# The first two-job unit of an expert stage gets the loop's fourteen steps, its pair products in the first step and its slots from a table

## What is computed

```
def moe_swiglu(hn, router_w, w1, w3, w2):
    ...
    logits = (t @ router_w).astype(jnp.float32)
    top_v, top_i = lax.top_k(logits, TOP_K)          # TOP_K = 2 of 8
    gates = jax.nn.softmax(top_v, axis=-1)
    ...
    for e in range(N_EXPERTS):
        out = out + gate_te[:, e:e + 1] * swiglu(t, w1[e], w3[e], w2[e])
```

## Time and profile before

| | us |
|---|---|
| median of 3 runs | 1252.86 |
| lowest, highest | 1252.4, 1255.4 |
| profiled execution | 1251.35 |
| its span | 1249.6 |
| first matmul of an expert unit | 403.75 from the span's start |

### The profile page before, as it was taken

How to read it: one execution, slowest core, us unless ns; L and a number is a source line. 1 busy time by engine, 2 the same in 40 slices (tenths; PEclk the granted TensorE clock), 3 DMA queues, 4 the chain that set the end, 5 groups by cost and what they waited for, 6 DMA issues and landing times.

```text
span 1249.6 us, 16988 instructions
## 1 busy us (share of the span) xinstructions
PE 1219.5 (98%) x6506; PEld 874.2 (70%) x6506; DVE 710.3 (57%) x854; ACT 576.8 (46%) x608; POOL 20.0 (2%) x54
## 2 busy tenths in 40 slices
PE   8999999999999999999999999999999999999997
PEld 7688999999879765556655655575655666565654
DVE  5976666654553755555554642664545646464645
ACT  2266656533564652444354441634445444454443
POOL 3200000000000000000000000000000000000000
PEclk9999999999999999999999999999999999999999
DMA  9433555523075789999999999999999999999993
GB/s 388 183 149 133 173 181 186 201 101 135 2 301 208 266 331 423 421 421 421 421 421 420 421 420 422 420 422 421 421 420 421 422 421 421 421 420 422 420 422 142
DMA packets 58019, 411.83 MB, mean 330 GB/s; under 512 B 6241, under 2 KB 6369, under 8 KB 9697
## 3 DMA queue, kind: packets, MB, share of 16 engines
q1 hardware_dynamic: 57776, 410.68, 80.8%
q10 hardware_dynamic: 144, 0.26, 0.1%
q0 software_dynamic: 32, 0.00, 0.0%
HBM read 409.87 MB, written 1.05 MB: 329 GB/s over the span
## 4 chain that ended last, share of the span: by engine, by line
PE 81%; DMA 7%; DVE 6%; ACT 3%; issue 2%; SPq 1%; DVEq 0%; ACTq 0%
PE banks L1144 21%; PE banks L1116 10%; PE banks L1117 10%; PE banks L838 9%; PE banks L1119 9%; DMA raw<-in_exp_dram 6%; PE banks L853 5%; DVE low L2135 3%; PE banks L728 2%; PE banks L954 2%; PE banks L773 2%; PE banks L1089 2%; PE banks L742 1%; ACT squares L1468 1%; PE banks L1124 1%
## 5 line engine op out<-in xcount | busy, mean ns | idle before, releaser
L2135 DVE TENSOR_TENSOR low<-raw,high 128x2048 fp32r<-128x2048 f32 x165 | 374.4, 2288 | 157.6 <-ACT high L1526 157.2
L1526 ACT ACTIVATE high<-raw 128x2048 fp32r<-128x2048 f32 x165 | 313.6, 1913 | 305.8 <-DMA raw<-in_exp_dram 169.1
L1144 PE MATMUL banks<-raw,x_full 128*64 128x512 f32 x896 | 198.1, 595 | 1.9 <-ACT x_full L1536 1.9
L1116 PE MATMUL banks<-high,x_high 128*128 128x512 f32 x448 | 179.2, 400 | 2.0 <-DVE low L2135 2.0
L1119 PE MATMUL banks<-high,x_low 128*128 128x512 f32 x448 | 174.6, 390 | 0.0
L1117 PE MATMUL banks<-low,x_high 128*128 128x512 f32 x448 | 174.4, 389 | 0.0
L1144 PEld LDWEIGHTS banks<-raw,x_full 128*64 128x64 f32 x896 | 62.3, 137 | 121.0 <-issue 121.0
L1144 PE MATMUL banks<-raw,h_full 128*64 128x512 f32 x448 | 102.3, 598 | 0.0
L1116 PEld LDWEIGHTS banks<-high,x_high 128*128 128x128 f32 x448 | 84.1, 188 | 21.1 <-DVE low L2135 3.8
L1116 PE MATMUL banks<-high,h_high 128*128 128x512 f32 x224 | 92.0, 411 | 5.6 <-DVE low L2135 4.3
L1117 PEld LDWEIGHTS banks<-low,x_high 128*128 128x128 f32 x448 | 84.2, 188 | 18.2 <-issue 1.4
(11 more groups left out here) (312 smaller groups left out, 1592.4 us busy)
## 6 DMA issues: line engine op xcount, KB each, us to landing
raw<-in_exp_dram SPq DMA_DIRECT2D x336, 1024.0 KB, 19.4
raw<-in_ff_dram SPq DMA_DIRECT2D x33, 1024.0 KB, 4.7
weights<-in_w_in_conv_dram SPq DMA_DIRECT2D x4, 1024.0 KB, 10.2
weights<-in_w_out_dram SPq DMA_DIRECT2D x2, 2048.0 KB, 25.4
weights<-in_w_qkv_dram SPq DMA_DIRECT2D x1, 4096.0 KB, 18.0
weights<-in_w_o_dram SPq DMA_DIRECT2D x1, 4096.0 KB, 12.2
weights<-in_w_in_pool_dram SPq DMA_DIRECT2D x1, 2048.0 KB, 19.1
weights<-in_w_qkv_dram SPq DMA_DIRECT2D x1, 2048.0 KB, 8.2
```

The lines of the kernel that those rows point to most:

```text
L1116: pe.matmul(dst, own_high[:, i, :], high[:, slot, w], start=first, stop=False)
L1144: mm = pe.matmul(PS[rows, bank, :], own[:, k, rows], raw[:, raw_slot[at[t]], w], start=first, stop=last)
L1526: act.activation(high[:, k % SPLIT, :], raw[:, raw_slot[at], :], ACT.Copy).then_inc(high_ready, 1)
L2135: dve.tensor_tensor(low[:, k % SPLIT, :], raw[:, raw_slot[full_at(p, job.side * UNITS + k)], :], high[:, k % SPLIT, :].bitcast(F32), ALU.s ...
```

## The change

The opening is gone. `prelude` is removed from PE, ACT and DVE, the first duo uses LOOP_STEPS like every other, and `ups` has a branch for the first job, which has no earlier job to bring back: it turns its own selection after the first unit and gathers the pair's tokens after the fourth. The first duo's steps 0 and 1 thus hold pair units of group 0.

The loads of the first duo are no longer in the order of the products. The first sixteen are still full units 0 to 15 (OPENING = 16), because the pair's experts aren't known; then come all others in the products' order. A table, `first_places`, gives each unit its slot: load i takes the slot of the unit that stands at place i - 14 of the products' order. It also counts how often each slot was filled, for the waits. The loop gets its own table, which goes on from the slots where the first duo ends. Apart from this, ten warm-up matmuls are added at the kernel's start, four between the transposes of the input and six behind them.

```
-    FIRST_STEPS = [(0, 2, None, 0), (0, 3, 0, 1), (0, 4, 1, None), (0, 5, None, 2), (0, 6, 2, None),
-                   (1, 0, None, 3), (1, 1, 3, None), (1, 2, None, 4), (1, 3, 4, None), (1, 4, None, 5),
-                   (1, 5, 5, 6), (1, 6, 6, None)]
     LOOP_STEPS = [(s // GROUPS, s % GROUPS, s // 2 if s % 2 else None, None if s % 2 else s // 2)
                   for s in range(2 * GROUPS)]
...
+    opening = [("full", k) for k in range(OPENING)]
+    first_loads = opening + [unit for unit in joint if unit not in opening]
+
+    def first_places():
+        slots, turns, count = {}, {}, [0] * RAW
+        for i, unit in enumerate(first_loads):
+            s = i if i < RAW else slots[joint[i - RAW]]
+            count[s] += 1
+            slots[unit], turns[unit] = s, count[s]
+        return [slots[unit] for unit in joint], [turns[unit] for unit in joint], count
...
+            def load_first():
+                full_jobs = [0]
+                for t in range(RAW, len(first_loads)):
+                    unit = first_loads[t]
+                    if t == OPENING:
+                        sp.wait_ge(pairs_ready, 1)
...
+                    wait_gone(FIRST_DUO, *joint[t - RAW])
+                    load_one(unit, first_slots[joint.index(unit)], two if t >= OPENING else None, full_jobs)
...
             keep_warm(6, 9)
             for i in range(4):
+                if i == 2:
+                    keep_warm(6, 4)
...
                 mm.then_inc(xT_done, 1)
+            keep_warm(6, 6)
...
-            prelude(FIRST, FIRST_DUO)
-            duo_steps(None, FIRST_DUO, 0, FIRST_STEPS[:7])
+            duo_steps(None, FIRST_DUO, 0, LOOP_STEPS[:7])
...
             def beside_pair(job, p, g, down, up):
 
+                if job is FIRST and g == 0:
+                    pe.wait_ge(selT_ready, by_nth(job, 1, 1))
+                    pe.wait_ge(acc_ready, 4)
                 for m, unit in enumerate(pair_units(down, up)):
                     pair_unit(job.duo, p, *unit)
                     if m == 0:
                         turn_full(job, g)
-                    if p and up == 0 and m == 1:
+                    if up == 0 and m == 1:
                         turn_sel_pair(job.duo)
```

More of the change, by code:

```diff
@@ L114, in ups_by, with joint_order @@
     def ups_by(p, step):
[L115 to L133, removed]
+        return sum(up is not None for _, _, _, up in LOOP_STEPS[:step])
+    def joint_order():
+        order = []
+        for side, g, down, up in LOOP_STEPS:
+            k = side * UNITS + 6 * g
+            order += [("full", k + n) for n in range(4)]
+            for unit in pair_units(down, up):
+                m = 2 * pair_order.index(unit)
+                order += [("pair", m), ("pair", m + 1)]
+            order += [("full", k + 4 + n) for n in range(2)]
+        assert sorted(order) == sorted([(part, k) for part in ("full", "pair") for k in range(2 * UNITS)])
+        return order
+    joint = joint_order()
+    opening = [("full", k) for k in range(OPENING)]
[7 more added lines that the diff above has]
+        return [slots[unit] for unit in joint], [turns[unit] for unit in joint], count
+    first_slots, first_turns, first_count = first_places()
+    loop_slots = [first_slots[len(joint) - RAW + t % RAW] for t in range(len(joint))]
+    loop_turns = [first_count[s] + t // RAW + 1 for t, s in enumerate(loop_slots)]
+    raw_slot = (first_slots, loop_slots)
     FF_RAW = [11, 12, 13]
@@ L550, in _ @@
             sp.dma_start(w_o[:, :, :], w_o_in).then_inc(wo_loaded, 16)
-            for t, (part, k) in enumerate(joints[0][:RAW]):
-                assert part == "full"
+            for t in range(RAW):
                 if t == 0:
@@ L563, in wait_gone @@
                     sp.wait_ge(pair_done, by_duo(duo, PAIR_UNITS, m + 1))
[L565 to L587, removed]
+            def load_one(unit, slot, two, full_jobs):
+                part, m = unit
+                if part == "full":
+                    load_unit(full_jobs[m // UNITS], stream.index(full_order[m % UNITS]), slot)
+                else:
+                    load_unit(two[m % 2], stream.index(pair_order[m // 2]), slot)
@@ new lines, in load_first @@
+            def load_first():
[4 more added lines that the diff above has]
+                        sp.wait_ge(pairs_ready, 1)
+                        two = [sp.value_load(jobs_i[0:1, 1, i:i + 1], min_val=0, max_val=NE - 1) for i in range(2)]
+                    if unit == ("full", UNITS):
+                        sp.wait_ge(jobs_ready, 1)
+                        full_jobs += [sp.value_load(jobs_i[0:1, 0, 0:1], min_val=0, max_val=NE - 1)]
+                    wait_gone(FIRST_DUO, *joint[t - RAW])
+                    load_one(unit, first_slots[joint.index(unit)], two if t >= OPENING else None, full_jobs)
@@ L588, in _, with load_duo @@
+            def load_duo(prev, duo, two, full_jobs):
+                for t, unit in enumerate(joint):
+                    wait_gone(prev if t < RAW else duo, *joint[t - RAW])
+                    load_one(unit, loop_slots[t], two, full_jobs)
+            load_first()
             n_loop = sp.value_load(jobs_i[0:1, 1, NJ:NJ + 1], min_val=1, max_val=MOST)
@@ L1143, in pair_unit @@
                         rows = slice(t * HALF, (t + 1) * HALF)
-                        mm = pe.matmul(PS[rows, bank, :], own[:, k, rows], raw[:, raw_slot[at[t]], w],
+                        mm = pe.matmul(PS[rows, bank, :], own[:, k, rows], raw[:, raw_slot[p][at[t]], w],
                                        start=first, stop=last)
@@ L1579, in change @@
                 if job.side:
-                    act.wait_ge(pair_turned, by_duo(job.duo, GROUPS, ups_by(p, DUO_STEPS[p].index(
-                        next(step for step in DUO_STEPS[p] if step[0])))))
+                    act.wait_ge(pair_turned, by_duo(job.duo, GROUPS, ups_by(p, LOOP_STEPS.index(
+                        next(step for step in LOOP_STEPS if step[0])))))
                 else:
```

134 lines of the change are left out of this document (39 added, 95 removed).

## The result

| | before | after |
|---|---|---|
| median of 5 runs, us | 1253.84 | 1276.46 |
| lowest, highest | 1252.4, 1255.4 | 1276.02, 1278.39 |
| ratio | | 1.0179 [1.0166, 1.0191] |
| profiled execution, us | 1251.35 | 1276.32 |
| its span | 1249.6 | 1274.6 |

The change makes the kernel 1.8% slower, 22.6 us by the medians and 25.0 us by the two profiled executions. The profiled execution before was 2.5 us quicker than its median, the one after 0.1.

A forecast was written before the change was run, and what follows sets the result against it. PE was taken as the bound from 404 us on, the DMA a close second. Gaps 22.8, clock 5.5, groups 0.6, warm-ups 0.3 and waits -4.0 made +25.2 us on 1252.9: 1278 us, range 1268 to 1286.

The forecast's parts named there:

- part 2: Step 0's pair units share two slots, so three load round trips of 8.0 us leave PE idle 22.8 us.
- part 3: PE's clock falls in the three gaps of step 0; three restarts cost 5.5 us, bounds 0 and 10.5.
- part 6: The DMA lags 19.9 us at load 25, less than PE, so late waits for data go: -4.0 us.
- PE is the bound, and the DMA a close second: From 404 us on PE's units stand shoulder to shoulder and set the time; the DMA is nearly full too.
- the DMA is the bound: Rival: PE catches up and the end moves by the DMA's lag, 1272.8 us, or 1267.4 without a clock fall; chance 0.17.
- parts 4, 5: Two more groups of pair units cost 0.6 us; ten warm-up matmuls at the start cost 0.3 us.
- Not slower: Rival: step 0's pair loads fill the DMA's lull; 1238.8 us if DMA alone bounds, 1249.8 if PE; chance 0.05.

The follow-up runs named there:

- e1: Changed kernel with fourteen full units loaded ahead instead of sixteen, so slots 0 to 3 go to pair loads: 1251.51 us, 0.9977 of the kernel before.
- e3: Changed kernel with thirty small dummy matmuls behind each of the first three pair units, filling the gaps: 1269.95 us, 1.0126 of the kernel before.
- e6: Kernel before with sixty small dummy matmuls in the middle of the first two-job unit: 1262.4 us, ratio 1.0067.
- e10: Kernel before with only the first half of each of the second duo's 168 loads brought: 1251.24 us, ratio 0.9977.
- e11: Kernel before with the second duo's loads halved and its full jobs' up units without high weights by low tokens: 1218.07 us, ratio 0.9712.
- e4: Changed kernel with twelve full units loaded ahead instead of sixteen, the pair's first loads into empty slots: 1250.56 us, 0.9968 of the kernel before.
- e8_open100: Kernel before with a hundred small dummy matmuls in the opening, behind the gather of the pair's tokens: 1277.19 us, ratio 1.0178.
- e9: Kernel before without the product of high weights by low tokens in the second duo's full-job up units: 1254.58 us, ratio 1.0001.
- e2: Changed kernel without the ten added warm-up matmuls at the start: 1275.93 us, 1.0176 of the kernel before.
- e7: Changed kernel with twelve full units loaded ahead instead of sixteen and without the ten warm-up matmuls: 1250.7 us, 0.9968 of the kernel before.
- e5: Kernel before with twenty small dummy matmuls in the middle of the first two-job unit: 1255.0 us, ratio 1.0002.

## Why the prediction was right, and where it was not

Forecast 1278 (1268 to 1286), measured 1276.46. The mechanism of the slowdown is as forecast; that the sum comes out within 2 us is in part luck. The clock cost 2.2 us more than forecast, and 2.4 us more of waits came back; the forecast shift of 25.2 stands against 22.6 by the medians, and against 25.0 by the profiles with 1.2 of it from the start. Point by point:

**The gaps (part 2): right in cause and size.** Forecast 22.8 us in three idle times of about 7, measured 22.0. The loads go out in twos behind a unit's end, and the unit starts 7.5, 7.7 and 8.1 us later, for a forecast of 8.0. That the slots do it, e1 shows: moving the two full loads out of them takes 25 us off. Two details were off: the DMA moved 154 GB/s from 424 to 465 us, not near 200, and the pairs of issues are 14 us apart, not 11 to 13, because a slow pair unit lies between.

**The clock (part 3): right in cause, too small.** Forecast 5.5, measured 7.7 in the rows and 6.5 by e3. I took the kernel's start as the model, where the half clock ends within 4.1 us. Here it lasts for most of a 6-us pair unit. Of the two bounds, 0 and 10.5 (each pair unit at half clock from end to end), the upper was the nearer to what one unit loses: 2.3 to 2.9 of 3.5.

**The DMA's lag (part 6): too small, and it turned out to be the better measure of the end.** Forecast 19.9 us, measured 24.3 at the 42nd load and 24.9 at the last. I counted it at load 25 with a clock term of 5.5 instead of 7.7 (2.2 of the difference) and left out the late start (1.2); the rest, about 1 us, fits a further short lull before the stream is full (the 33rd and 34th loads land 3.6 and 3.5 us behind the one ahead of each, the eight behind them 2.5). In all but e6, e10 and e11 the span ends 756 to 758 us behind the landing of the 42nd load, whatever happened ahead of it:

| | 42nd load landed | last load landed | span |
|---|---|---|---|
| before | 493.1 | 1228.4 | 1249.6 |
| after | 517.4 | 1253.3 | 1274.6 |
| e1_open14 | 492.1 | 1227.9 | 1249.2 |
| e3_warm_gaps | 511.6 | 1246.8 | 1268.1 |
| e4_open12 | 490.6 | 1225.4 | 1246.7 |
| e8_open100 | 519.6 | 1254.6 | 1275.8 |
| e9_less_pe | 499.2 | 1234.3 | 1255.5 |

**"PE is the bound, and the DMA a close second": half right.** The spacing of the units did tell that PE is full (e10), against the share of the weight loads. But I set the DMA second, and e9 shows that it is no second: 51 us of PE's work taken away gave nothing. The rival "the DMA is the bound" named that mechanism and came out 4 to 9 us short (1272.8, 1267.4) because its lag was mis-sized; with the measured 24.9 and the start's 1.2 off it gives 1252.9 + 23.7 = 1276.6, which shows that it fits, not that it alone is true. With both full, the end follows whichever lags more, and in this change they lag by nearly the same.

**What comes back (part 6): 6.4, not 4.0.** I had counted three of the five waits for a split (4.0 of 4.9); the wait for `x_full` (1.9) and one for `area_c` (0.7) went too, and 1.1 stayed.

**Warm-ups and the two more groups (parts 4, 5): small, as forecast, but not measured.** The warm-ups were to push the projection 0.3 us late; it waits for its weights as before, and e2 and e7 find no difference in the time. For the two groups, forecast at 0.6, there is only the 0.5 that the rows leave over.

**Not slower: refuted for this change, true of its idea.** The rival held that the pair products could fill the DMA's lull if their loads had slots. They don't here. In e4 they do, and then the gain is 4.0 us. I had put the prize at 14 us where the DMA alone sets the end; e4's own opening has a lull too (222 GB/s), only an earlier one.

What stays open: e6 costs 8.4 us by its ratio and 9.8 by its rows, within the interval; what the 0.5 us left over consists of; and why e11 gives 36 us of 51.

## What to carry to other kernels

Where loads go through a ring of slots, list for each load who releases its slot and when, above all for the first steps after a change of order: units that are loaded early and used late close the ring for what is needed now, and one number (16 or 14 loads ahead) was worth 25 us here. Before a resource is called second, take work off the first and see: here each of the two, relieved alone, gave 0 to 3 us, and both together 36. Idle times on TensorE can be paid with the clock on top; here each of 7 to 8 us cost another 2.3 to 2.9, and the one of 3.25 in e1 another 1.6.

## What the runs showed of the hardware

- The granted clock fell to 0.50 inside each of three idle times of 6.9 to 8.1 us and stayed there for most of the pair unit behind: 6.53, 6.24 and 5.90 us for work that takes 3.65 at 1.00.
- Shorter waits brought the fall too, and the length of one wait did not tell it. Behind the 3.25 us of e1, a wait of 2.43 us in e10 (to 785.62) and one of 1.92 us in e5 (to 1208.77) the clock fell to 0.50; the kernel before has a wait of 2.04 us and stays at 1.00. The stretch behind the wait in e5, with PE busy throughout:

```profile
1209.30:1212.60 3.30, 3.30 (x9) 2.51 (x9) 3.30 (x4) 1.91 (x1) 0.00 (x0) 0.50 1.01 422
```

- In e9 the mean clock over 860 to 1200 us is 0.98, though no wait of PE there is longer than 3.0 us. The waits of e9 in that stretch:

```profile
PE banks L1116 <- DVE low L2138: 18.5, 24, 3.0
```

- From the 42nd load on the stream has no gap that matters in any kernel with full loads and little stall: a load of 1 MB every 2.50 us on average, the last lands 21.2 to 21.9 us before the end.
- From the issue of the first of two loads into an empty queue to the start of the matmul behind both it took 7.4 to 7.9 us; the 42nd load, in the full stream, takes 11.7 (12.7 before) from issue to landing. The answer on the DMA for the load issued at 505.9 us in the changed kernel (KB, median us):

```profile
raw<-in_exp_dram SPq DMA_DIRECT2D x1, 1024.0 KB, 11.7
```
